# A vector step that corrects the RWKV queries, moved by one slot in a two-layer hybrid decoder kernel

## The chip, the cores and the metric

The kernel runs on one core of a Trainium2 chip. The metric is the device time of one execution in microseconds (us); it includes a short stretch before the first and after the last profiled instruction. The engines of the core are TensorE (PE; its weight loads are shown apart, as PEld), VectorE (DVE), ScalarE (ACT), GpSimd (POOL) and SyncE (SP, which here only issues DMAs). Each takes its instructions in the order in which they are written, and they meet through semaphores.

## The reference

The reference is a trunk of two layers over 512 positions of width 1024. In each layer the normed input goes through one projection whose columns belong to four groups of heads: RWKV-7 time mixing, a short gated convolution, block-sparse attention (MoBA), and RetNet retention. Each group's output is multiplied by a SiLU gate, and one output projection follows. The part that matters here is the RWKV recurrence of each head:

```
def step(state, inp):
    r_t, w_t, k_t, v_t, kk_t, a_t = inp
    s_kk = jnp.einsum('bhij,bhj->bhi', state, kk_t)
    state = (state * w_t[:, :, None, :]
             - s_kk[..., None] * (kk_t * a_t)[:, :, None, :]
             + v_t[..., None] * k_t[:, :, None, :])
    y_t = jnp.einsum('bhij,bhj->bhi', state, r_t)
    return state, y_t
```

All arithmetic is in float32.

## The kernel before

Each layer is one written order of steps (`STEPS`, made by `layer_steps`, lines 142 to 204). Every engine walks through the same list and issues its own part of each step, so the list sets the order of every engine's queue; an engine that has no part in a step skips it. Nothing reorders the work on the chip.

The projections are cut into tiles of 128 columns. A projection of 512 positions takes 24 matmuls of 128x512 (a high and a low part of the activations and the weights, three products for each of eight parts of the depth, L769 to L772). Sixteen of them, from ret_g0 to conv_g1, are cut into quarters, and small steps are put between. This part of the layer has 32 slots. Slot i issues quarter 2(i mod 2) of its projection, then the list `mid[i]`, then the next quarter, and, on odd slots, the step that reads the finished projection, then the list `after[i]` (lines 196 to 200). Slot 15 ends the projection moba_g1; slots 16 and 17 make up the projection cc0.

The recurrence is computed in chunks of 64 positions. `chunk_q` (PE, L1095) multiplies the matrices W with a part of the score matrix into two jobs in PSUM, q0 in bank 6 and q1 in bank 5. `queries` (DVE only) adds them to the rho part of AR and releases the two banks:

```
for c in range(2):
    dve.wait_ge(*full(f"q{c}", layer))
    ...
    for odd in range(2):
        ...
        ins = tt(to, to, q[:, :, :, odd, :], ALU.add)
    ins.then_inc(done(f"q{c}", layer), 1)
```

`chunk_y1` (PE, L1100 and L1101, in `mid[17]`) starts the outputs y0 in bank 5 and y1 in bank 6. Through `begin` (line 715) it waits until all former readers of a bank have released it. `chunk_y` (`after[19]`) adds the part that reads the corrected rho. `chain` c carries the state from one chunk to the next, PE L1117 and then DVE L1897.

The attention works in six units a layer. For unit u, `attend_scores` runs on PE (L1005), then on DVE (bias L1813, maximum L1818, for two heads), then on ACT (exponential L1451); `attend_norm` on DVE takes the reciprocal of the sum (L1825) and scales (L1828), and `attend_turn` transposes the result on PE (L1016), and ACT copies it (L1457); `attend_values` follows on PE (L1032). Unit 2 has its scores in `after[15]`, its norm in `mid[16]` and its turn in `mid[17]`.

In order, the list around the change reads, by slot: in slot 15 quarter 2 of moba_g1, chain 3, chunk_q, **queries**, attend_turn 1, quarter 3, the gate of moba_g1 (ACT L1356, DVE L1748), attend_values 1, chain 4, attend_scores 2; in slot 16 quarter 0 of cc0, attend_norm 2, quarter 1; in slot 17 quarter 2, chain 5, chunk_y1, attend_turn 2, quarter 3, then conv_c 0, attend_values 2, attend_out 0, chain 6, attend_scores 3.

Of the kernel before, what the change touches and what calls it, by code (L numbers as in the profile page):

```python
# [141 lines left out]
def layer_steps():  # L142

    s = [("k_pair",)]
    s += [("shift", "k0"), ("shift", "k1"), ("kk_input",), ("shift", "wa"), ("shift", "r0"), ("kk_square",),
          ("kk_norm",), ("kk_unit", 0), ("lora_tanh",), ("shift", "r1"), ("kk_unit", 1), ("lora",), ("shift", "v0"), ("decay_scan",), ("shift", "v1"),
          ("decay_exp",), ("factors", 0), ("gate", "rwkv", 0), ("factors", 1), ("gate", "rwkv", 1), ("factors", 2)]

    s += [("copy", "rq0"), ("copy", "rq1"), ("bonus",), ("rotate", "rq0"),
          ("copy", "rk0"), ("rotate", "rq1"), ("scores", 0), ("scores", 1), ("copy", "rk1"), ("rotate", "rk0"), ("to_rows", "v"), ("scores", 2),  # L150
          ("scores", 3), ("wide", 0, 0), ("wide", 0, 1), ("rotate", "rk1"), ("wide", 0, 2), ("wide", 0, 3),
          ("to_rows", "kap"), ("to_rows", "bet"), ("block_rows", 0), ("wide", 1, 0), ("wide", 1, 1), ("wide_out", 0), ("wide_out", 1),
          ("to_rows", "alp"), ("block_rows", 1), ("wide", 1, 2), ("wide", 1, 3), ("wide_out", 2), ("wide_out", 3), ("to_rows", "rk"),
          ("block_rows", 2)]

    last = [("gate", "ret", 0), ("gate", "ret", 1)] + [("copy", j) for j in ("mq0", "mk0", "mq1", "mk1")] + [("gate", "moba", 0), ("gate", "moba", 1)]
    last += [("conv_c", 0), ("conv_c", 1), ("conv_h", 0), ("conv_h", 1), ("conv_b", 0), ("conv_b", 1), ("gate", "conv", 0), ("gate", "conv", 1)]
    slots = 2 * len(last)  # L160
    mid, after = [[] for _ in range(slots)], [[] for _ in range(slots)]
    after[0] += [("retain_state",), ("retain_scores", 0), ("retain_scores", 1)]
    after[1] += [("centre_v",), ("inverse_eye",)]
    after[2] += [("retain_values",), ("retain_out", 0), ("retain_out", 1)]
    after[5] += [("ret_low",)]
    for i, step in [(INV0, ("inverse_x",)), (INV0, ("chunk_b",)),
                    (INV0 + 1, ("inverse_y",)), (INV0 + 1, ("inverse_yt",)),
                    (INV0 + 3, ("corner_x",)), (INV0 + 4, ("corner_t",)), (9, ("ret_stat",)), (10, ("chunk_uw",)),
                    (11, ("chunk_gh",)), (17, ("chunk_y1",)), (21, ("ln_square",)), (22, ("ln_var",))]:
        mid[i].append(step)  # L170
    for c in range(1, NCH - 1):


        if c % 2:
            mid[12 + c].insert(0, ("chain", c))
    after[9] += [("ret_root",), ("ret_recip", 0)]
    for u in range(UNITS + 1):


        if u > 0:  # L180
            mid[11 + 2 * u].append(("attend_turn", u - 1))
            after[11 + 2 * u].append(("attend_values", u - 1))
            if u % 3 == 0:
                after[11 + 2 * u].append(("attend_out", u // 3 - 1))
        if u in (1, 2, 3):
            after[11 + 2 * u].append(("chain", 2 * u))
        if u < UNITS:
            (after[11 + 2 * u] if u else mid[10]).append(("attend_scores", u))
            (mid[12 + 2 * u] if u else after[11]).append(("attend_norm", u))
    mid[15][1:1] = [("chunk_q",), ("queries",)]  # L190
    after[19].append(("chunk_y",))
    for i, step in [(10, ("ret_recip", 1)), (11, ("ret_recip", 2)), (12, ("ret_recip", 3)), (13, ("ret_finish", 0)), (14, ("ret_finish", 1)),
                    (21, ("conv_taps", 0)), (24, ("conv_taps", 1)), (22, ("ln_recip", 0)), (23, ("ln_recip", 1)), (25, ("ln_recip", 2)), (26, ("ln_recip", 3)),
                    (26, ("ln_scale", 0)), (27, ("ln_scale", 1)), (28, ("rwkv_finish", 0))]:
        after[i].append(step)
    for i in range(slots):
        step, job = last[i // 2], project_name(last[i // 2])
        s += [("quarter", job, 2 * (i % 2))] + mid[i] + [("quarter", job, 2 * (i % 2) + 1)]
        if i < slots - 1:
            s += [step] * (i % 2) + after[i]  # L200

    s += [("split_y", k) for k in Y_ORDER[:4]] + [("rwkv_finish", 1), ("split_y", 0), last[-1], ("conv_out", 0), ("split_y", 1), ("conv_out", 1)]
    s += [("split_y", k) for k in Y_ORDER[6:]] + [("out", q) for q in range(5)] + [("out_end",)]
    return s
# [5 lines left out]
def project_name(step):  # L210

    kind = step[0]
    if kind == "gate":
        return f"{step[1]}_g{step[2]}"
    if kind in ("conv_c", "conv_h", "conv_b"):
        return {"conv_c": "cc", "conv_h": "ch", "conv_b": "cb"}[kind] + str(step[1])
    return step[1]


Y_ORDER = [6, 7, 4, 5, 0, 1, 2, 3]  # L220
ROW_ORDER = [3, 2, 0, 1]
STEPS = layer_steps()


# [1871 lines left out]
```

## Time and profile before

| what | value |
|---|---|
| median of 3 runs | 582.1 us (582.08 to 582.6) |
| the profiled execution's own time | 582.1 us |
| its span, first to last instruction | 580.3 us |
| DVE busy | 368.2 us (63%) |
| ACT busy | 275.2 us (47%) |
| POOL busy | 250.0 us (43%) |
| mean granted clock of TensorE | 0.997 |
| data moved | 64.61 MB, 111 GB/s |

The busy time is the sum of the stretches in which an engine has an instruction in work. Matmuls are pipelined and their ends are modelled, so a busy PE is not PE at its peak. In the timelines that follow a row is a group of equal instructions: start, length, engine, line, operation, output and inputs, shapes and count. A bracket at its end gives the time for which the engine stood idle ahead of it, and what ended that time; "issue" there means that nothing in the profile shows what it waited for.

### The profile page before, as it was taken

What the parts mean: (1) busy time and instruction counts of PE and PEld (TensorE: products, weight loads), DVE (VectorE), ACT (ScalarE), POOL (GpSimd) and SP (SyncE); (2) the same over time, 40 slices, a digit from 0 to 9 for tenths busy, and PEclk for the clock granted to TensorE, in tenths of its full rate; (3) what the DMA queues carried; (4) which work ended last, traced back from release to release, by engine and by line L of the source; (5) the groups of instructions that cost most, each with busy time, mean ns of one, the idle gap of its engine ahead of it and who ended that gap; (6) DMA issues with size and microseconds to landing.
All of it is one profiled execution on the core that took longest, in us unless ns stands there. A gap on an engine that the chain in (4) does not pass through costs nothing. (4 is left out here: it accounts for less than half of the span.)

```text
span 580.3 us, 12191 instructions
## 1 busy us (share of the span) xinstructions
PE 571.3 (98%) x4988; PEld 466.8 (80%) x4988; DVE 368.2 (63%) x624; ACT 275.2 (47%) x551; POOL 250.0 (43%) x197
## 2 busy tenths in 40 slices
PE   9999999999999999999999999999999999999995
PEld 7978888888777777888898788888878777788884
DVE  4999975582277557774444897936424874778163
ACT  6485331345273475534657643324537335745253
POOL 5846451046922313436335555402385313145340
PEclk9999999999999999999999999999999999999998
DMA  9557625055422121354544433422644121224513
GB/s 279 163 152 207 205 74 119 0 134 142 110 76 73 38 73 56 111 175 137 159 125 130 110 85 98 110 46 88 141 118 113 37 75 38 72 73 146 182 41 141
DMA packets 103371, 64.61 MB, mean 111 GB/s; under 512 B 29151, under 2 KB 94227, under 8 KB 103188
## 3 DMA queue, kind: packets, MB, share of 16 engines
q1 hardware_dynamic: 103316, 63.83, 39.5%
q8 instruction: 40, 0.66, 0.5%
q14 instruction: 15, 0.12, 0.1%
HBM read 55.68 MB, written 8.14 MB: 110 GB/s over the span
## 5 line engine op out<-in xcount | busy, mean ns | idle before, releaser
L703 POOL TENSOR_TENSOR w_lo<-w_raw,w_hi 128x512 fp32r<-128x512 f32 x156 | 217.8, 1416 | 290.2 <-ACT w_hi L1282 284.7
L769 PE MATMUL bank<-act_hi,w_hi 128*128 128x512 f32 x432 | 173.1, 401 | 0.0
L772 PE MATMUL bank<-act_lo,w_hi 128*128 128x512 f32 x432 | 168.4, 390 | 0.4 <-issue 0.4
L771 PE MATMUL bank<-act_hi,w_lo 128*128 128x512 f32 x416 | 162.3, 390 | 0.0
L1282 ACT ACTIVATE w_hi<-w_raw 128x512 fp32r<-128x512 f32 x140 | 80.2, 620 | 73.7 <-PE bank L854 28.2
L769 PEld LDWEIGHTS bank<-act_hi,w_hi 128*128 128x128 f32 x432 | 81.1, 188 | 25.0 <-issue 8.5
L772 PEld LDWEIGHTS bank<-act_lo,w_hi 128*128 128x128 f32 x432 | 81.1, 188 | 18.1 <-issue 0.9
L771 PEld LDWEIGHTS bank<-act_hi,w_lo 128*128 128x128 f32 x416 | 78.2, 188 | 14.7
L1208 PE MATMUL bank<-w_hi,act_hi 128*128 128x512 f32 x128 | 50.0, 391 | 0.0
L1210 PE MATMUL bank<-w_hi,act_lo 128*128 128x512 f32 x128 | 49.8, 389 | 0.0
L1209 PE MATMUL bank<-w_lo,act_hi 128*128 128x512 f32 x128 | 49.8, 389 | 0.0
L1981 DVE TENSOR_TENSOR x_or_y<-x_or_y,bank 128x512 f32<-128x512 f32 x16 | 10.9, 686 | 38.1 <-PE bank L1210 38.1
L1390 ACT ACTIVATE pages<-bank 128x512 f32<-128x512 f32 x16 | 9.5, 596 | 42.4 <-PE bank L772 42.3
L1210 PEld LDWEIGHTS bank<-w_hi,act_lo 128*128 128x128 f32 x128 | 24.0, 188 | 5.1
L1209 PEld LDWEIGHTS bank<-w_lo,act_hi 128*128 128x128 f32 x128 | 24.0, 188 | 4.9
L1208 PEld LDWEIGHTS bank<-w_hi,act_hi 128*128 128x128 f32 x128 | 24.0, 188 | 4.9
L1451 ACT ACTIVATE pages<-pages,small 128x128 f32<-128x128 f32 (+3 forms) x32 | 17.9, 558 | 19.0 <-DVE small L1818 19.0
L852 PE MATMUL bank<-w_hi,act_hi 128*128 128x512 f32 x64 | 25.5, 398 | 0.0
L854 PE MATMUL bank<-w_hi,act_lo 128*128 128x512 f32 x64 | 25.0, 390 | 0.0
L853 PE MATMUL bank<-w_lo,act_hi 128*128 128x512 f32 x64 | 24.9, 390 | 0.0
L1748 DVE SCALAR_TENSOR_TENSOR x_or_y<-x_or_y,bank 128x512 f32<-128x512 f32 x16 | 10.9, 684 | 21.1 <-ACT x_or_y L1356 20.8
L1356 ACT ACTIVATE x_or_y<-bank 128x512 f32<-128x512 f32 x16 | 9.6, 599 | 31.0 <-PE bank L772 31.0
(217 smaller groups left out, 951.2 us busy)
## 6 DMA issues: line engine op xcount, KB each, us to landing
w_raw<-in_w_in_dram SPq DMA_DIRECT2D x62, 512.0 KB, 4.1
w_raw<-in_w_out_dram SPq DMA_DIRECT2D x16, 512.0 KB, 3.7
pages<-in_x_dram SPq DMA_DIRECT2D x4, 512.0 KB, 6.1
x_or_y<-in_x_dram SPq DMA_DIRECT2D x4, 512.0 KB, 4.0
x_scratch<-x_or_y SPq DMA_DIRECT2D x4, 512.0 KB, 2.9
x_or_y<-x_scratch SPq DMA_DIRECT2D x4, 512.0 KB, 3.8
out_dram<-pages SPq DMA_DIRECT2D x8, 256.0 KB, 2.2
bias_scratch<-pages SPq DMA_DIRECT2D x1, 1280.0 KB, 8.2
```

The costliest lines, as they stand in the source:

```text
L703: ins = pool.tensor_tensor(low, raw, w_hi[:, i % HI, k, 0:n].bitcast(F32), ALU.subtract)
L769: mm(b[:, :], hi, act_hi[:, k, :], start=n == 0, stop=False)
L771: mm(b[:, :], lo, act_hi[:, k, :], start=False, stop=False)
L772: ins = mm(b[:, :], hi, act_lo[:, k, :], start=False, stop=n == KT - 1)
L852: mm(o, act_hi[:, n, tc], w_hi[:, :, n, :], start=n == 0, stop=False)
L853: mm(o, act_hi[:, n, tc], w_lo[:, :, n, :], start=False, stop=False)
L854: ins = mm(o, act_lo[:, n, tc], w_hi[:, :, n, :], start=False, stop=n == KT - 1)
L1208: mm(b[:, :], act_hi[:, k, tc], hi[:, wc], start=first, stop=False)
L1209: mm(b[:, :], act_hi[:, k, tc], lo[:, wc], start=False, stop=False)
L1210: ins = mm(b[:, :], act_lo[:, k, tc], hi[:, wc], start=False, stop=last)
L1282: go(w_hi[:, i % HI, k, 0:n], w_raw[:, i % RAW, k, 0:n], ACT.Copy).then_inc(s("w_high"), 1)
L1451: go(pb, pb, ACT.Exp, bias=row_max[:, n:n + 1], accum_out=row_sum[:, n:n + 1]).then_inc(s("prob"), 1)
```

## The change

`queries` is taken out of the middle of slot 15, where it stood behind `chunk_q`, and is appended to `mid[16]`. When that line runs, `mid[16]` holds `attend_norm` 2, so `queries` stands behind it: the list now reads quarter 0 of cc0, attend_norm 2, queries, quarter 1. `chunk_q` stays where it was. Nothing else differs; line numbers below the place grow by one.

```diff
-    mid[15][1:1] = [("chunk_q",), ("queries",)]
+    mid[15].insert(1, ("chunk_q",))
+    mid[16].append(("queries",))
     after[19].append(("chunk_y",))
```

## Rows read from the trace of the kernel before

**Rows 1.** The page, busy us, share of the span and instructions.
```profile
PE 571.3 (98%) x4988; PEld 466.8 (80%) x4988; DVE 368.2 (63%) x624; ACT 275.2 (47%) x551; POOL 250.0 (43%) x197
```

**Rows 2.** Waits of PE, whole span: us in total, times, longest us.
```profile
PE bank L1098 <- issue: 1.0, 1, 1.0
PE bank L737 <- POOL pages L677: 1.0, 1, 1.0
PE bank L772 <- issue: 0.4, 1, 0.4
```

**Rows 3.** Timeline of DVE, layer 1, slots 15 to 17.
```profile
467.01 0.69 DVE L1836 SCALAR_TENSOR_TENSOR x_or_y<-pages,x_or_y 128x512 f32<-128x512 f32 x1
467.62 0.47 DVE L1897 SCALAR_TENSOR_TENSOR pages<-bank,chunk_decay,pages 128x64 f32<-128x64 f32 x2
468.00 1.40 DVE L1890 TENSOR_TENSOR pages<-pages,bank 128x256 f32<-128x256 f32 x4
470.20 0.69 DVE L1748 SCALAR_TENSOR_TENSOR x_or_y<-x_or_y,bank 128x512 f32<-128x512 f32 x1 [0.80 <-ACT x_or_y L1356]
...
471.64 0.69 DVE L1813 SCALAR_TENSOR_TENSOR pages<-bank,bias 128x512 f32<-128x512 f32 x1 [0.37 <-PE bank L1005]
...
475.26 0.17 DVE L1825 RECIPROCAL small<-small 128x1 f32<-128x1 f32 x1 [0.29 <-ACT pages L1451]
475.46 0.49 DVE L1828 TENSOR_SCALAR pages<-pages,small 128x512 f32<-128x512 f32 x1
476.31 0.48 DVE L1897 SCALAR_TENSOR_TENSOR pages<-bank,chunk_decay,pages 128x64 f32<-128x64 f32 x2 [0.37 <-PE bank L1117]
...
481.75 0.69 DVE L1836 SCALAR_TENSOR_TENSOR x_or_y<-bank,x_or_y 128x512 f32<-128x512 f32 x1 [4.96 <-PE bank L1032]
```

**Rows 4.** Timeline of ACT, layer 1, end of the exponentials of unit 2.
```profile
475.04 0.19 ACT L1451 ACTIVATION_READ_ACCUMULATOR pages<-pages,small 128x1 f32 x1
```

**Rows 5.** Timeline, layer 1, a DVE scale and the PE weight load behind it.
```profile
504.46 0.49 DVE L1828 TENSOR_SCALAR pages<-pages,small 128x512 f32<-128x512 f32 x1
...
505.01 0.42 PEld L1016 LDWEIGHTS bank<-constants,pages 128*128 128x128 f32 x4 [0.21 <-DVE pages L1828]
```

**Rows 6.** Timeline of PE and its weight loads, layer 1, slot 17.
```profile
475.81 0.45 PE L1117 MATMUL bank<-pages 64*64 64x64 f32 x8
476.04 0.25 PEld L1100 LDWEIGHTS bank<-pages 64*64 64x64 f32 x6
...
478.21 0.85 PEld L1016 LDWEIGHTS bank<-constants,pages 128*128 128x128 f32 x8
...
481.63 0.30 PEld L1117 LDWEIGHTS bank<-pages 64*64 64x64 f32 x7 [0.17 <-issue]
```

**Rows 7.** Timeline of DVE, layer 0, end of attend_norm 2.
```profile
194.19 0.49 DVE L1828 TENSOR_SCALAR pages<-pages,small 128x512 f32<-128x512 f32 x1
```

**Rows 8.** Timeline of PE's weight loads, layer 0, start of chunk_y1.
```profile
194.77 0.25 PEld L1100 LDWEIGHTS bank<-pages 64*64 64x64 f32 x6
```

**Rows 9.** Waits of PE's weight loads, whole span: total, times, longest.
```profile
PEld bank L1032 <- ACT pages L1457: 1.1, 2, 0.5
...
PEld bank L1016 <- DVE pages L1828: 0.8, 4, 0.2
```

**Rows 10.** PE behind a gap; windows: PE, PEld, DVE, ACT, POOL, PEclk, DMA, GB/s.
```profile
169.93 0.27 PE L1098 MATMUL bank<-pages 64*64 64x64 f32 x1 [1.00 <-issue]
...
170.00:200.00 30.00, 30.00 (x392) 23.15 (x394) 20.37 (x50) 11.34 (x25) 7.68 (x6) 1.00 0.21 54
```

**Rows 11.** Weight loads behind the scores of units 1 and 2, layer 1.
```profile
461.65 0.19 PEld L769 LDWEIGHTS bank<-act_hi,w_hi 128*128 128x128 f32 x1 [0.60 <-issue]
...
471.50 0.19 PEld L769 LDWEIGHTS bank<-act_hi,w_hi 128*128 128x128 f32 x1 [0.81 <-issue]
```

**Rows 12.** The same matmuls at the start of the span and later.
```profile
0.99 2.08 PE L737 MATMUL bank<-pages 128*128 128x128 f32 x8 [0.99 <-POOL pages L677]
...
11.01 1.06 PE L737 MATMUL bank<-pages 128*128 128x128 f32 x8
```

## The prediction

> **What bounds the kernel now.** I began with the page. TensorE (PE) is busy 571.3 of 580.3 us, and the next engine, VectorE (DVE), 368.2 us [rows 1]. A pipelined PE that is called busy need not be at its peak, so I then asked for PE's waits: the three longest of four come to 2.4 us in the whole span, none of them in the stretch that the change touches, and none is for a weight tile in that stretch [rows 2]. So the order on PE sets the end: whatever makes PE stand still is paid in full unless a later wait of PE shrinks by it, and work taken off DVE gains nothing while DVE is not what PE waits for. That makes this a question about one release, and who needs what `queries` writes, and when. From there on I read only the timelines of DVE and PE around slots 15 to 17 of each layer.
>
> **The edit.** `queries` runs on DVE alone: four additions of a bank into the rho half of AR, c=0 from job q0 (bank 6), c=1 from q1 (bank 5). Their last one of each bank releases it. It has two kinds of users: `chunk_y`, behind slot 19, reads the sums; and `chunk_y1`, in the middle of slot 17, writes y0 into bank 5 and y1 into bank 6, and asks for both releases before its first matmul. The instructions are the same before and after, and so are the banks, the PE order (`queries` has no PE, ACT, POOL or SP part; it issues no DMA and passes none), and the weights' path. Only DVE's order changes: `queries` goes from behind chain 3 to behind `attend_norm` 2. DVE takes its queue in order, so it is now behind the gate of moba_g1, chain 4, the eight large steps of attention unit 2, and with them behind two ScalarE (ACT) exponentials.
>
> **What leaves its old place.** The four additions take 1.40 us from 468.00 to 469.40 [rows 3]. Behind them DVE stands idle 0.80 us for ACT's half of the gate, whose own start is set by the projection on PE. So the gate's second half stays at 470.20, chain 4 follows, and the first step of unit 2 at 471.64 waits 0.37 us for PE's scores [rows 3]. Gain: 0. The 1.40 us were in idle time, which covers them wholly (1.40 + 0.80 us free before 470.20). Layer 0 has the same order of steps.
>
> **Where it comes back.** The last instruction of `attend_norm` 2 starts at 475.46 and takes 0.49; its predecessor waited 0.29 us for the second exponential's sum, which ends at 475.23 [rows 3, 4]. This chain (PE scores, add bias, maximum, exponential, reciprocal, scale) starts from PE's scores, so it does not move when DVE is freed earlier. `queries` can therefore start only when that scale is let through. How near may two DVE instructions stand? The row of chain 3 starts 0.08 before the end of the one ahead of it (467.01 + 0.69 = 467.70 against 467.62) and the additions start 0.09 before the end of chain 3 [rows 3]. I take 0.09: start 475.95 - 0.09 = 475.86. At the cautious end is the scale itself, which waits for its reciprocal and starts 0.03 after that one's end (475.26 + 0.17 = 475.43 against 475.46): start 475.98. The four additions then end at 475.86 + 1.40 = 477.26. PE's release by DVE has a row too: a scale that ends at 504.46 + 0.49 = 504.95 lets PE's weight load go at 505.01, so 0.06 us [rows 5]. `chunk_y1` starts at 477.32.
>
> Before, its first weight load is at 476.04, straight behind chain 5, with nothing to wait for: the bank had been free since 469.40 [rows 3, 6]. So PE loses 477.32 - 476.04 = **1.28 us** in layer 1 (with the cautious start 1.40). Layer 0: 194.19 + 0.49 - 0.09 + 1.40 + 0.06 = 196.05 against 194.77, again **1.28 us** [rows 7, 8]. PE has two wait instructions here, one for each bank, and the later bank (5) is asked for first; the second is met by then and should cost between nothing and the 0.06 of one release; I call it 1.3 a layer. Sum: 2 x 1.3 = 2.6 us.
>
> **What is late next.** Queued behind the waiting `chunk_y1` on PE: its 128 small matmuls of 17 ns (476.04 to 478.21 [rows 6]), the transposes of unit 2, and all the rest of the layer. Chain 5 stands ahead of it and is not held. On DVE, chain 5's two steps stood at 476.31 and now come behind `queries`, at 477.2; chain 6 on PE needs them, at 481.63 before, and DVE has 4.96 us of idle ahead of 481.75 [rows 3, 6]. That cover holds; without it, chain 6 would pay 0.9 us. ACT's next step is the copy of PE's transposes, which moves with PE. So no second delay.
>
> **Does a later wait give it back?** PE's waits after slot 17 are small: for ACT's copy of turned probabilities 0.5 us of weight-load idle in each layer, and for DVE's scale 0.2 twice in each layer [rows 9]. Both waits are for work that itself starts from PE in the same stretch, so it shifts with PE, and they don't shrink. If they all did, 0.9 us a layer would come back, 0.8 us of cost would remain over both layers. The weight stream (DMA, ACT, POOL) runs from releases by PE, and PE doesn't wait for it, so its slack only grows. I take 0 given back.
>
> The profiled execution itself took 582.1 us, of which 580.3 are the span and 1.8 lie around it; that is also the median of the runs, so no shift between the two is needed: 582.1 + 2.6 = **584.7 us**.
>
> **Two rules of the Trainium skill.** The first is about the clock. The rows: at 169.93 PE had stood idle 1.00 us (1.13 us for weight loads), and the granted clock of the 30 us after it is 1.00 [rows 10]; the new gap, from the end of chain 5's matmuls (475.81 + 0.45 = 476.26 [rows 6]) to 477.32, is 1.06 us, so the same size. The skill's page "TensorE: Matmul & The Clock Gate", section "HAM oscillation — how this bites in real kernels", tells that a wait between bursts of matmuls can send the clock back to its lower level, so that the next burst starts cold. By the rows there is no such cost; by that rule there could be, and it is a rival below.
>
> The second is about DVE. The rows show the four additions of 0.41 us each within 1.40 us, so they overlap by 0.08 us apiece [rows 3]. "VectorE: DVE Perf Modes", section "The DRAIN you can't avoid", says that after each operation the pipe has to empty before the next may start, though the page lets an instruction that is not held start earlier. By the rows of before the cost is 1.28 us a layer, by that rule it would be larger, which is a rival too.
>
> **Rivals.**
> 1. *Faster.* Place: DVE between 468.0 and 471.6. If PE's gap behind the scores of unit 2 were DVE's doing, an earlier DVE would close it. It is 0.81 us there against 0.60 us behind the narrower scores of unit 1 [rows 11]; the difference of 0.21 us is the price, 0.4 us in two layers: 581.7. It decides only if `queries` is also done before PE gets to `chunk_y1`, so if `attend_norm` 2 ended 1.3 us earlier than it does. Against it: the gap is put down to issue and grows with the width of the matmul, and the exponentials' chain hangs on PE. 4%.
> 2. *Hidden.* `queries` slips into DVE's idle time ahead of 475.46 (0.37 + 0.29 us), or PE's delay is absorbed by later waits. For it: PE has such waits. Against: the idle comes to 0.66 us for 1.40 us of work in an in-order queue, and the order in which the slot lists are filled puts `attend_norm` 2 first. 582.1 to 583.0. 5%.
> 3. *DVE without overlap.* The additions start at 475.98 and take 4 x 0.41 = 1.64, PE goes on 0.06 later at 477.68: 1.64 us a layer, 3.3 in all, 585.4. Against: the same four took 1.40. 3%.
> 4. *The clock falls in the new gap.* At PE's start, eight matmuls take 2.08 us that take 1.06 us at 11.0 [rows 12]: twice as long. If that held for the stretch from `chunk_y1` to chain 6 (476.04 to 481.63, 5.6 us [rows 6]), it would add 5.6 us a layer: 584.7 + 11.2 = 595.9. Against: the gap of the same size above, at full clock. 2%.
> The forecast itself: 86%.
>
> **How the numbers follow.** The forecast's own spread: the start of `queries` (0.12 us a layer), the second wait on PE (0.06), the small give-back (up to 0.3 a layer, since it can't be excluded wholly), and 0.5 us of spread between the runs of before. 584.7 thus runs from 583.8 to 585.4; rival 3 is at its upper edge, and 1, 2 and 4 stay outside. Range 583.7 to 585.6. A difference under 0.2% (1.2 us) can't be told from no change in this kernel: slower 0.86 + 0.03 + 0.02 = 0.91, same 0.05, faster 0.04.
>
> **What would show it.** In the new profile: the four additions of L1891 (L1890 before) directly behind the last scale of unit 2, near 194.6 in layer 0 and near 477.2 in layer 1, which by then is 1.3 us late as a whole; the gate of moba_g1 in layer 0 where it was; a wait of PE or its weight loads at `chunk_y1` (L1101 after) put down to DVE's additions, about 1.1 us of idle twice; PE's busy time as before; the clock at 0.997; the later waits of rows 9 unchanged. Wrong would be: no idle ahead of `chunk_y1` (then the release wasn't late), an idle of 1.1 us but the end less than 2 us later (then a later wait gave it back, and it must be smaller), or a gap elsewhere on PE that wasn't there.

## The result, and the profile after

| | before | after |
|---|---|---|
| median | 582.59 us (582.08 to 582.87, 5 runs) | 585.61 us (584.31 to 586.02, 5 runs) |
| ratio after / before | | 1.0052, 95% interval 1.0037 to 1.0066 |
| the profiled execution | 582.1 us, span 580.3 | 585.21 us, span 583.4, clock 0.996 |

The change makes the kernel 3.0 us slower. The forecast was 584.7 us in 583.7 to 585.6, with 2.6 us for the change. The direction and the two pauses came as forecast; the time is 0.9 us above the forecast and 0.01 us beyond the upper end of its range.

Line numbers of the changed kernel are one higher. The waits of TensorE (line waited at, what released it, us in total, times, longest) have a new first entry; those of its weight loads (PEld) come second. [rows 2, 9] answer to them.

```profile
PE bank L1101 <- DVE pages L1891: 2.1, 2, 1.1
PE bank L738 <- POOL pages L678: 1.0, 1, 1.0
PE bank L1099 <- issue: 0.7, 1, 0.7
PE bank L773 <- issue: 0.5, 1, 0.5
```
```profile
PEld bank L1101 <- DVE pages L1891: 2.4, 2, 1.2
...
PEld bank L1033 <- ACT pages L1458: 1.1, 2, 0.5
```

The page's busy times answer to [rows 1]. PE's rose by 1.4 us, where the prediction had it unchanged; 0.65 us of this is a slower start of this one execution (see below).

```profile
PE 572.7 (98%) x4988; PEld 468.0 (80%) x4988; DVE 368.5 (63%) x624; ACT 275.4 (47%) x551; POOL 250.2 (43%) x197
```

The timeline of DVE, first layer 0 and then layer 1, in the slots of [rows 3, 7]:

```profile
189.28 0.69 DVE L1749 SCALAR_TENSOR_TENSOR x_or_y<-x_or_y,bank 128x512 f32<-128x512 f32 x1 [2.12 <-ACT x_or_y L1357]
...
194.54 0.49 DVE L1829 TENSOR_SCALAR pages<-pages,small 128x512 f32<-128x512 f32 x1
194.95 1.41 DVE L1891 TENSOR_TENSOR pages<-pages,bank 128x256 f32<-128x256 f32 x4
196.27 0.47 DVE L1898 SCALAR_TENSOR_TENSOR pages<-bank,chunk_decay,pages 128x64 f32<-128x64 f32 x2
...
473.46 0.69 DVE L1814 SCALAR_TENSOR_TENSOR pages<-bank,bias 128x512 f32<-128x512 f32 x1 [0.37 <-PE bank L1006]
...
477.07 0.17 DVE L1826 RECIPROCAL small<-small 128x1 f32<-128x1 f32 x1 [0.29 <-ACT pages L1452]
477.27 0.49 DVE L1829 TENSOR_SCALAR pages<-pages,small 128x512 f32<-128x512 f32 x1
477.68 1.41 DVE L1891 TENSOR_TENSOR pages<-pages,bank 128x256 f32<-128x256 f32 x4
479.00 0.47 DVE L1898 SCALAR_TENSOR_TENSOR pages<-bank,chunk_decay,pages 128x64 f32<-128x64 f32 x2
```

The additions stand directly behind the last scale of unit 2. In their old place is only more idle: 2.12 us ahead of the gate's second half, where 0.80 us were left. The waits of unit 2 are what they were, 0.37 us for the scores and 0.29 us for the exponential [rows 3]. PE and its weight loads at `chunk_y1`, layer 0 and then layer 1, answer to [rows 6, 8]:

```profile
194.90 0.31 PEld L1118 LDWEIGHTS bank<-pages 64*64 64x64 f32 x8 [0.35 <-issue]
196.41 0.23 PEld L1101 LDWEIGHTS bank<-pages 64*64 64x64 f32 x8 [1.20 <-DVE pages L1891]
...
477.63 0.31 PEld L1118 LDWEIGHTS bank<-pages 64*64 64x64 f32 x8 [0.35 <-issue]
479.14 0.23 PEld L1101 LDWEIGHTS bank<-pages 64*64 64x64 f32 x8 [1.20 <-DVE pages L1891]
```
```profile
477.63 0.45 PE L1118 MATMUL bank<-pages 64*64 64x64 f32 x8
479.14 0.37 PE L1101 MATMUL bank<-pages 64*64 64x64 f32 x8 [1.06 <-DVE pages L1891]
```

From the start of chain 5 to that of `chunk_y1` the weight loads now take 479.14 - 477.63 = 1.51 us; they took 476.04 - 475.81 = 0.23 [rows 6], so they lose the forecast 1.28 us a layer. The matmuls themselves lose a little less, since before the change the first one of `chunk_y1` started 0.05 us behind its weight load (PE, kernel before):

```profile
476.09 0.33 PE L1100 MATMUL bank<-pages 64*64 64x64 f32 x6
```

That makes 1.51 - 0.28 = 1.23 us a layer for PE. The idle of 1.06 us is the forecast 477.32 - 476.26. From the start of the last scale to PE's start 1.87 us pass in both layers (194.54 to 196.41, 477.27 to 479.14), where 1.86 were forecast.

### The profile page after: what moved, and what is told of

Its sections match the earlier page's. It is cut to its first block and busy times, and to the rows that moved or that the text cites. A ratio compares the mean times of both kernels' runs of the same rounds, so it can differ in the third digit from the quotient of the medians.

```text
span 583.4 us, 12191 instructions
## 1 busy us (share of the span) xinstructions
PE 572.7 (98%) x4988; PEld 468.0 (80%) x4988; DVE 368.5 (63%) x624; ACT 275.4 (47%) x551; POOL 250.2 (43%) x197
```

## The experiments

The edits are against the kernel before, if nothing else is said. To see where time goes, I set the matmuls of two traces side by side, first with first, second with second, and read the interval between the starts of neighbours; "pause" below is such an interval. Where `chunk_y1` isn't late, the one at its start is 0.05 us, so a pause of 1.28 us costs 1.23.

**The two kernels again.** Nothing edited; two full comparisons of the change, one of the kernel before with itself, and four single profiled executions.

> The changed kernel again, unaltered. In the profiles PE loses 1.23 and 1.28 us ahead of chunk_y1 in the two layers, 2.5 us together, while the whole span grew by 3.1. Theory A (the release by queries is all the change does, and the rest differs from one execution to the next): the two gaps come out at 1.28 us again to a hundredth or two, the part of the span outside them varies by some tenths of a us in either direction, and the median difference to the kernel before is 2.5 us give or take 0.4 (585.1, ratio 1.0043). Theory B (the change costs more than the two gaps, somewhere else and in each execution): the span outside the gaps is again 0.5 to 0.6 us longer than before, at the same places, and the difference of the medians stays at 3.0 or more.

> The changed kernel a third time, on the same chip as the other runs of this call. Theory A: PE's two pauses ahead of chunk_y1 at 1.28 us between matmuls against 0.05 before, 2.46 us together, and a ratio of 1.0042 to 1.0053. Theory B: the transposes of unit 2 in layer 0 again have a gap of several tenths, and the ratio is over 1.005.

> The kernel before against itself, to see what a comparison of equal programs gives and how much single executions differ. In the profiles so far PE's time outside the change's gaps varies at four fixed places: the end of the slow clock at the start (0 to 0.75 us), the gap within the last matmuls of chunk_gh in layer 0 (0.87 to 1.48 between two matmuls), one matmul of the transposes of unit 2 in layer 0 (0.11 to 0.73) and one projection matmul in layer 1 (0.82 to 1.13). Theory A (these vary by themselves): the profile of this run shows values inside those ranges, and the ratio is 1.0000 within 0.0007, though a bias up to 0.001 would then also be a matter of chance. Theory B (the change or its variants widen them): all four are near the small values of the first profile of before (0.11 for the transposes), and the ratio is 1.0000, so that the 0.1% of the variants is theirs.

> The changed kernel, one more profile. Theory A: gap at the transposes of unit 2 in layer 0 between 0.2 and 0.75. Theory B: as often as not near 0.11, and the gap in layer 1 (0.82 or 1.13) takes either value.

> The kernel before, one more profile. Open: the time of the changed kernel is 3.0 to 3.1 us above before in three comparisons, while its two pauses in the profile come to 2.46 us and the slower start of the burst to 0.1. Theory A (the other 0.5 us is in the gap of the transposes of unit 2 in layer 0, which the late burst makes likelier): before shows 0.11 to 0.22 there again, the changed kernel 0.2 to 0.7. Theory B (independent of the change): before shows such a gap of over 0.4 in some profile too.

> The changed kernel once more, for its pauses. Both theories: 1.28 us at chunk_y1 in each layer. Theory A (the rest of the difference is the pause inside the transposes of unit 2 in layer 0, longer with the change): that pause is above 0.3 us. Rival (chance): it is about 0.1 us, as in the kernel before, and the profiled time is then near 585.2 us.

> The kernel before once more. Theory A: the pause inside the transposes of unit 2 in layer 0 is 0.1 to 0.2 us, as in its profiles so far. Rival (chance): it is now and then 0.5 us or more here too.

The change measured 585.69 us (585.4 to 586.38) against 582.72, ratio 1.0053 (1.0039 to 1.0067), and 585.84 us against 582.81, ratio 1.0053 (1.0040 to 1.0065). The kernel before against itself (control_before): 582.85 us, ratio 1.0001 (0.9992 to 1.0010). The single executions: after 585.15 twice, before 583.17 and 582.69. The cost is some 3.0 us in each of three comparisons, and the level of the kernel before is 582.6 to 582.8, not 582.1.

Set side by side, the five profiles of the change and four of the kernel before differ like this (us, means of the profiles):

| term | before | after | difference |
|---|---|---|---|
| pause at `chunk_y1`, both layers | 2 x 0.05 | 2 x 1.28 | 2.46 |
| from its first matmul to that of the next step, both layers | 2 x 2.12 | 2 x 2.17 | 0.10 |
| pause inside the transposes of unit 2, layer 0 | 0.11, 0.22, 0.11, 0.11 | 0.19, 0.73, 0.47, 0.19, 0.19 | 0.22 |
| start, to the 42nd matmul behind the first | 12.24 to 12.75 | 12.05 to 12.89 | 0.08 |
| span | 580.9 | 583.8 | 2.9 |

The first four rows come to 2.86 of the 2.9 us. Two other pauses vary from run to run as much in the one kernel as in the other: one inside `chunk_gh` of layer 0 (1.14 to 1.62 before, 0.90 to 1.62 after) and one inside a projection in layer 1 (0.84 to 1.40, 0.80 to 1.13). The third row shows in the timelines of PE, first in the changed kernel's second profile (control_after), where it is long:

```profile
199.04 0.87 PE L1017 MATMUL bank<-constants,pages 128*128 128x128 f32 x6
200.37 0.38 PE L1017 MATMUL bank<-constants,pages 128*128 128x128 f32 x2 [0.46 <-issue]
```

and then in its last one (after_d), where the seven records run on without idle:

```profile
198.55 1.00 PE L1017 MATMUL bank<-constants,pages 128*128 128x128 f32 x7
199.31 0.47 PE L770 MATMUL bank<-act_hi,w_hi 128*128 128x512 f32 x1
```

So the expectation that this pause is above 0.3 us with the change failed in the last profile (0.19 us, as in two others), and the time there was 585.15, as the rival said. Yet it isn't chance alone. In the eight profiles of kernels that keep all or half of `queries` in slot 15 (four of the kernel before, and four of the versions below), this pause is 0.11 us seven times and 0.22 us once. In the eight at full clock with all four additions later and `chunk_y1` in slot 17, it is 0.19 us three times and 0.47 to 0.73 us five times. So the moved additions lengthen it, by an amount that varies from run to run; why is not shown.

**The same step ahead of the norm.** (Run front16.) If lateness is all, `queries` can stand in slot 16 as long as it is done before PE comes.

```diff
-    mid[15][1:1] = [("chunk_q",), ("queries",)]
+    mid[15].insert(1, ("chunk_q",))
+    mid[16].insert(0, ("queries",))
```

> queries also leaves slot 15 for slot 16, but stands ahead of attend_norm 2 instead of behind it. Theory A: by the trace of before it starts 0.09 before the end of the last maximum of unit 2 (473.69 + 0.69 = 474.38), so at 474.29, and ends at 475.69; PE asks for the banks at 476.04, so there is no gap and the time is that of before (ratio 1.0000, difference under 0.3 us). attend_norm 2 then ends near 477.1, still ahead of its transposes at 478.2. Theory B (a move out of slot 15 costs by itself): still 0.5 us or more above before. A theory that takes the slot rather than the neighbour as the cause expects 2.5 us.

> queries ahead of attend_norm 2 again, one more profile. Its first profile had a gap of 0.72 at the transposes of unit 2 in layer 0 though PE had not waited before them. If that gap is only tied to the lateness of PE, it is 0.11 to 0.22 this time; if it differs from run to run in every kernel, either is possible; if it is tied to the new order on DVE, 0.7 again.

Measured 583.22 us (582.17 to 584.36), ratio 1.0010 (1.0001 to 1.0019); the second profiled execution 583.20. The additions fill the idle in which DVE waited for the exponentials, and PE finds its bank free (DVE, then PEld):

```profile
194.07 1.40 DVE L1891 TENSOR_TENSOR pages<-pages,bank 128x256 f32<-128x256 f32 x4
195.40 0.16 DVE L1826 RECIPROCAL small<-small 128x1 f32<-128x1 f32 x1
```
```profile
195.60 0.31 PEld L1118 LDWEIGHTS bank<-pages 64*64 64x64 f32 x8 [0.35 <-issue]
195.82 0.25 PEld L1101 LDWEIGHTS bank<-pages 64*64 64x64 f32 x6
```

Both pauses are gone, and with them some 2.5 of the 3.0 us. What is left is 0.5 to 0.6 us (0.1 to 1.1 by the interval). That is the size by which the pause inside the transposes of unit 2 grew: 0.72 us in both profiles, here with no lateness of PE at all:

```profile
199.32 0.38 PE L1017 MATMUL bank<-constants,pages 128*128 128x128 f32 x2 [0.45 <-issue]
```

**Half of the step moved.** (Run half_late.) The additions of q0 stay, those of q1 go behind the norm.

```diff
+    mid[15][1:1] = [("chunk_q",), ("queries", 0)]
+    mid[16].append(("queries", 1))
...
-                    for c in range(2):
-                        dve.wait_ge(*full(f"q{c}", layer))
+                    dve.wait_ge(*full(f"q{c}", layer))
```

> queries cut in two: the additions of bank 6 stay in slot 15, only those of bank 5 go behind attend_norm 2. Theory A (the cost is how long PE waits for the later release, not that there is one): start 475.86, two additions 0.33 + 0.41, release 0.06, so PE goes on at 476.66 instead of 476.04: 0.6 us in each layer, 1.2 us together; ratio 1.0021, half of the changed kernel's. A cost fixed for each late release would leave 2.5 us.

Measured 583.84 us (583.04 to 584.38), ratio 1.0019 (1.0010 to 1.0027). The two additions behind the scale take 0.75 us, and the pause is 0.62 us in each layer, 0.66 less than with four:

```profile
195.04 0.75 DVE L1890 TENSOR_TENSOR pages<-pages,bank 128x256 f32<-128x256 f32 x2
```
```profile
195.84 0.23 PEld L1101 LDWEIGHTS bank<-pages 64*64 64x64 f32 x8 [0.53 <-DVE pages L1890]
```

2 x 0.57 + 0.10 = 1.24 us against 1.0 to 1.1 measured. The cost follows the time at which the last addition ends. By the code `chunk_y1` asks for both banks before its first matmul, so the other half should be no freer to move; no run shows that.

**The step even later.** (Run behind_chain5.) Behind DVE's part of chain 5.

```diff
-    mid[15][1:1] = [("chunk_q",), ("queries",)]
+    mid[15].insert(1, ("chunk_q",))
+    mid[17].insert(1, ("queries",))
```

> queries one step later still on DVE, behind the two additions of chain 5 (476.31 to 476.79 before). Theory A: start 476.70, end 478.10, PE released at 478.16 against 476.04, so 2.12 us of delay in each layer, 4.2 us together: 586.8 with a before of 582.6, ratio 1.0073. A clock that falls in the longer gap (1.9 us of idle) would show a granted clock under 1.00 behind it and matmuls of the burst at twice their 17 ns, over 2 us more in each layer. A delay that later waits give back in part would leave less than twice the gap.

> The layout with the additions behind unit 5's chain once more. Theory A: a pause of 2 us at chunk_y1 followed by small matmuls lets the granted clock fall in layer 0 again (0.50 for some 3 us, 1.6 us lost): time near 588 us. Rival: the fall was a chance of one run; the clock stays at 1 and the time is near 586.8 us.

Measured 588.01 us (587.07 to 588.36), ratio 1.0090 (1.0076 to 1.0103); the second profiled execution 586.91. The pause is 2.12 us in both layers, in both profiles, so 2 x 2.07 = 4.14 us, and 0.10 for the slower steps behind it, which is about what the second one shows. The first profile has more. The start of its `chunk_y1` in layer 0, windows around and behind it (PE, PEld, DVE, ACT, POOL busy, granted clock, DMA share, GB/s), and the transposes behind `chunk_y1`:

```profile
197.08 0.37 PE L1101 MATMUL bank<-pages 64*64 64x64 f32 x8 [1.90 <-DVE pages L1891]
```

```profile
196.90:198.20 1.30, 1.12 (x70) 1.12 (x74) 0.14 (x2) 0.00 (x0) 0.00 (x0) 1.00 0.05 13
198.30:201.60 3.30, 3.30 (x74) 3.18 (x67) 0.00 (x0) 0.42 (x1) 0.00 (x0) 0.50 0.00 0
201.70:205.00 3.30, 3.30 (x48) 2.48 (x46) 0.63 (x2) 2.30 (x5) 0.41 (x1) 1.00 0.03 5
```
```profile
200.03 1.88 PE L1017 MATMUL bank<-constants,pages 128*128 128x128 f32 x8
```

The granted clock fell to half (1.2 of 2.4 GHz) in layer 0 only, when PE had stood idle 1.90 us and then run small matmuls for 1.2 us, and stayed there for 3.4 us. Side by side with a profile without the fall, that cost about 1.6 us. In the second profile of the same kernel, with the same pause, it stayed up in the same place:

```profile
198.30:201.60 3.30, 3.10 (x83) 2.73 (x76) 0.00 (x0) 1.20 (x2) 0.00 (x0) 1.00 0.00 0
```

So the fall is real and doesn't come each time. The page "TensorE: Matmul & The Clock Gate" of the Trainium skill, section "HAM oscillation — how this bites in real kernels", says that a wait between bursts of matmuls can bring the clock down for the next burst; the first profile agrees, with its 0.50, and the second, at 1.00, did without. With the idle of 1.06 us of the change under study, none of five profiles shows a fall at this place.

**The consumer later too.** (Run y1_later.) The change, and `chunk_y1` in slot 18 instead of 17.

```diff
-                    (11, ("chunk_gh",)), (17, ("chunk_y1",)), ...
+                    (11, ("chunk_gh",)), (18, ("chunk_y1",)), ...
```

> The changed kernel, with chunk_y1 moved on by one slot on PE (from slot 17 to 18); queries stays late, behind attend_norm 2. Theory A (the cost is the wait of chunk_y1 for the two banks and nothing else): the banks are free at 477.3, chunk_y1 is asked for some 3 us of PE work later, so no gap; time as before, 582.6, ratio 1.0000 within 0.0007. If the late queries or the later chain 5 on DVE cost something of their own, the time stays above before by 0.5 us or more.

Measured 583.41 us (583.09 to 584.3), ratio 1.0015 (1.0006 to 1.0024). The wait is gone, as every theory said, but the time isn't back at that of before. PE in slot 18:

```profile
201.03 0.23 PEld L1101 LDWEIGHTS bank<-pages 64*64 64x64 f32 x8 [0.36 <-issue]
```

In slot 17 `chunk_y1` came straight behind chain 5, small matmuls behind small ones. In slot 18 it stands alone between wide projection matmuls. From the first matmul of chain 5 to that of the scores of unit 4, PE takes 13.97 us instead of the 13.58 of the kernel before in each layer, 0.78 us together, of which the 0.36 us ahead of the first load is the visible part. I had not reckoned with that. (Chain 5 had the same 0.35 us of issue ahead of it when it opened the small steps.)

**Can the order be improved?** (Run turn_first.) In the kernel before, PE waits 0.5 us a layer for ACT's copy at L1032 [rows 9]. Moving ln_square behind attend_turn 4 lets ACT copy first.

```diff
-        ... (21, ("ln_square",)), (22, ("ln_var",))]:
+        ... (22, ("ln_var",))]:
...
+    mid[21].append(("ln_square",))
```

> The kernel before with ln_square put behind attend_turn 4 in slot 21, so that ACT copies the turned probabilities of unit 4 before the four squares of the layer norm and not behind them; aimed at the wait of PE for ACT that stays in both kernels. Theory A (order of a queue sets when a release comes, here to our gain): the weight loads of attend_values 4 wait 0.3 us for issue, as at the other units, instead of 0.5 for ACT; PE gains 0.2 us in each layer, 0.4 together, ratio 0.9993 (hardly measurable in time, plain in the profile). Rival: ACT's squares, now 1 us later, hold up the copies of a weight tile and the exponentials of unit 5, and PE waits longer for DVE's scales at the next transposes (0.2 before): no gain or a loss of some tenths.

Measured 583.89 us (582.87 to 585.68), ratio 1.0019 (1.0010 to 1.0028): slower. The wait became 0.35 us of issue, 0.23 us gained a layer, and a longer one came at the transposes of unit 5, 0.70 us a layer. With ACT's squares later, a step of DVE that needs them came later too, and behind it in DVE's order the whole of unit 5: its reciprocal, with the taps of the convolution ahead of it in both kernels, moved from 504.27 to 505.55, while chain 5 on PE moved only from 475.81 to 476.61. PE's weight loads:

```profile
498.68 0.64 PEld L1033 LDWEIGHTS bank<-pages 128*64 128x64 f32 x12 [0.35 <-issue]
...
506.29 0.42 PEld L1017 LDWEIGHTS bank<-constants,pages 128*128 128x128 f32 x4 [0.89 <-DVE pages L1829]
```

**The taps moved as well.** (Run both_moved.) On top of turn_first, conv_taps 0 goes from slot 21 to slot 22, behind ln_recip 0.

```diff
-        (21, ("conv_taps", 0)), ..., (22, ("ln_recip", 0)), (23, ...
+        ..., (22, ("ln_recip", 0)), (22, ("conv_taps", 0)), (23, ...
```

> The kernel before with two moves: ln_square behind attend_turn 4 (as in turn_first, where it won 0.23 us a layer at attend_values 4 and lost 0.62 at the transposes of unit 5), and conv_taps 0 behind attend_norm 5 and ln_recip 0 on DVE, so that the 1.5 us of conv_taps no longer stand ahead of the reciprocal of unit 5. Theory A: in turn_first the loss came from DVE's queue: the bias step of unit 5 and with it conv_taps were 1.3 us late, and the reciprocal stood behind them. Without conv_taps ahead, the last scale of unit 5 ends near 504.4 on the clock of before, ahead of its transposes at 505.0, so PE neither loses the 0.62 nor the 0.08 that before loses there: gain 0.23 + 0.08 a layer, 0.6 us together, ratio 0.9990. Rival: the exponentials of unit 5, not conv_taps, set the scale, or conv_taps is now late for conv_b: no gain.

Measured 582.83 us (582.53 to 583.43), ratio 1.0002 (0.9993 to 1.0011). Unit 5's transposes wait no more, but its values wait for a copy that stands behind ACT's table load and square roots of ln_var (ACT, then PEld):

```profile
504.56 1.28 ACT L1529 ACT_TABLE_LOAD   x1
505.86 1.26 ACT L1529 ACTIVATE pages<-bank,units 128x512 f32<-128x512 f32 x2
507.01 1.08 ACT L1458 ACTIVATE pages<-bank 128x512 f32<-128x512 f32 x2
```
```profile
508.21 0.88 PEld L1033 LDWEIGHTS bank<-pages 128*64 128x64 f32 x16 [0.93 <-ACT pages L1458]
```

**And the square roots moved.** (Run three_moved.) On top of both_moved, ln_var goes from slot 22 to slot 23, behind attend_turn 5, and ln_recip 0 goes to slot 23 with it.

```diff
-        ... (17, ("chunk_y1",)), (22, ("ln_var",))]:
+        ... (17, ("chunk_y1",))]:
+    mid[23].append(("ln_var",))
...
-        ..., (22, ("ln_recip", 0)), (22, ("conv_taps", 0)), (23, ...
+        ..., (22, ("conv_taps", 0)), (23, ("ln_recip", 0)), (23, ...
```

> The kernel before with three of layer steps moved: ln_square behind the transposes of unit 4, the taps of the convolution behind the reciprocal of unit 5's normalisation, and the variance's square roots on ScalarE behind the transposes of unit 5 instead of ahead of the copy of its values. Theory A: the 0.59 us a layer that TensorE lost at the values of unit 5 in the version with two moved steps came from the table load and the two square roots ahead of the copy; with them behind it the wait goes, and the 0.23 + 0.14 us a layer won earlier stay: 0.7 us less than before in all, ratio 0.9988. Rival: the reciprocal of the variance or the layer's next step, now later, becomes the next wait and eats the gain: ratio 1.000 or above, with an idle of TensorE put down to ScalarE or VectorE behind unit 5.

Measured 582.80 us (582.27 to 583.75), ratio 1.0005 (0.9996 to 1.0014). The copy is early (the first half at 505.99), yet the gain is not there: with ln_var's four matmuls gone from ahead of them, the transposes of unit 5 come sooner, and now wait for both scales (PEld, then DVE; line numbers two higher than before):

```profile
505.30 0.42 PEld L1018 LDWEIGHTS bank<-constants,pages 128*128 128x128 f32 x4 [0.23 <-DVE pages L1830]
506.27 0.42 PEld L1018 LDWEIGHTS bank<-constants,pages 128*128 128x128 f32 x4 [0.56 <-DVE pages L1830]
```
```profile
505.54 0.16 DVE L1827 RECIPROCAL small<-small 128x1 f32<-128x1 f32 x1 [0.29 <-ACT pages L1453]
505.73 0.49 DVE L1830 TENSOR_SCALAR pages<-pages,small 128x512 f32<-128x512 f32 x1
```

That scale waits for its exponential, so each of the three edits moved the wait to another member of the chain of unit 5. No version beat the kernel before.

## Why the prediction came out as it did

- **What bounds the kernel, and what leaves the old place (gain 0).** Right. DVE's idle ahead of the gate grew from 0.80 to 2.12 us and nothing got faster; the gate stands at 189.28 in layer 0, 0.35 us later than in the profile of before (188.93), which is that run's later start: its first 42 matmuls took 0.65 us more and its pause in `chunk_gh` 0.31 us less.
- **Where it comes back (1.28 us a layer).** Right for the weight loads in both layers, and the pause between PE's matmuls is 1.28 us in each of five profiles. But 0.05 us of it were there before, so this term measures 1.23 us: the forecast set PE's new start against the old start of its weight loads. The overlap of 0.09 us with the scale ahead, 1.40 us for the four additions (1.41 measured) and 0.06 us for the release all held. half_late and behind_chain5 changed only the time at which the last addition ends, and the pause went to 0.62 and 2.12 us.
- **The second wait (up to 0.06).** Not seen as an idle of its own; but the steps from `chunk_y1`'s first matmul on took 0.05 us more in each layer wherever it was late. The term was called 0.02 a layer and measured 0.05, which all but makes up for the 0.05 of the term above: 1.28 against 1.3 us a layer. That the sum of the two came out so near is in part luck.
- **What is late next.** Right: chain 5's additions on DVE come at 479.00, and nothing waited for them.
- **No give-back.** Right: the waits for ACT's copy stay at 1.1 us in two [rows 9]. What the prediction hadn't got is a further cost: the pause inside the transposes of unit 2 in layer 0 grew by 0.22 us on the average, and front16 shows that the new order can bring 0.6 us of it without any lateness. The sign that the prediction named for being wrong, "a gap elsewhere on PE that wasn't there", is half met: the gap was there before, but shorter.
- **The sum, which is the step that failed.** "That is also the median of the runs, so no shift between the two is needed: 582.1 + 2.6" took one execution at the low end of the kernel's runs as its level. In the comparison it ran at 582.59, so 0.49 of the 0.91 us by which the time was missed are in the base. The other 0.42 are the size of the change, 3.02 instead of 2.6: the two pauses with the slower steps behind them measured 2.56, the transposes 0.22, and the remaining 0.24 (0.08 of it in the start) lie inside the interval of the ratio, which is 0.8 us to either side; the runs can't tell them from chance. The range held 0.5 us for the spread between runs, but took that from three of them and laid it around a base that was itself at their lower edge; in the comparison of the kernel before with itself, 27 executions ran from 582.19 to 583.39 us. With 582.59 for the base the same sum gives 585.2.
- **The rivals.** Faster (DVE's earlier idle closing PE's gaps) and hidden: neither; nothing was absorbed. DVE without overlap: out, the additions took 1.41 us, not 1.64. The clock: it didn't fall at the pause of 1.06 us, the gap of the same size in the profile of before [rows 10] was the right guide. Its price was too high, too: at a pause twice as long the clock fell once, for 3.4 us and 1.6 us of time, not for the whole stretch to chain 6.

## What to carry to other kernels

When PE is the bound and its order is fixed, the price of moving a step on another engine can be read from three rows: what ends last ahead of its new place, its own length, and the start of its first user on PE; that sum gave PE's start to 0.01 us here. Ask for the first user, not the obvious one: the sums were needed in slot 19, but the bank they were read from was needed in slot 17. And take the base from many runs, not from the one that was profiled: 0.5 us of base counts as much as 0.5 us of effect.

## What the runs showed of the hardware

- **PE pauses with nothing to wait for, at fixed places.** Inside steps made of many small instructions PE stood still with "issue" as the cause, always at the same matmul, for a time that varied from run to run: 0.87 to 1.62 us inside `chunk_gh` of layer 0, 0.11 to 0.73 us inside the transposes of unit 2 in layer 0, 0.68 to 1.40 us in a projection of layer 1. The second one was 0.72 us in both profiles with the additions ahead of the norm, 0.11 in three of four of the kernel before, and 0.11 with `chunk_y1` moved. At 0.11 us it is no more than the interval between its neighbours. What sets these pauses isn't known.
- **One more change between wide and small matmuls cost 0.39 us.** y1_later moved the same 128 small matmuls between wide ones and lost that much in each layer, with no wait for another engine. That the change of width is the cause is argued from this one version.
- **The clock at the start.** The same matmuls run at half speed until 9.9 to 12.9 us from run to run, which is worth up to 0.95 us between two executions of kernels with the same start (12.05 to 13.00 us to the 42nd matmul). This and the pauses above are most of the spread: the four profiles of the kernel before differ by 1.1 us in their spans, and by less than 0.3 us in what is left without them.
- **The clock can fall behind an idle of 1.90 us of PE, and need not:** once in two profiles, and only in one of two layers. In none of the other 17 profiles did it fall between the start and the last 5 us of the span.
